# Embedding of the four prompt tiles: one pass by column quarters in place of two passes by tile pairs

## What is computed

```python
def finish_layer(x, mla_o, gla_o, p_i, w):
    mix = jnp.concatenate([rmsnorm(mla_o, w["norm_mla_out"]), gla_o], -1) @ w["w_out"]
    h = x + mix
    h = h + peer(rmsnorm(h, w["norm_ffn"]), w)
    gate = jax.nn.sigmoid((rmsnorm(h, w["norm_ple"]) @ w["w_ple_gate"]).astype(F32)).astype(h.dtype)
    return h + gate * (p_i @ w["w_ple_proj"])
```

## Time and profile before

| | |
|---|---|
| median of 3 runs | 4336.06 us |
| span of the profiled execution | 4331.6 us |
| VectorE busy | 3288.1 us, 76% |
| TensorE busy | 2254.9 us, 52% |
| DMA moved | 1599.51 MB, mean 369 GB/s |
| gathered rows taken up | 1152 |

### The profile page before, as it was taken

The page is one execution under the profiler, slowest core; times in us unless marked ns, Lnnn a source line. Parts: engine busy times, 40 slices in busy tenths (PEclk is TensorE's granted clock), DMA queues, the critical chain, the costliest instruction groups (busy, mean ns, idle before and its releaser), DMA issues.

```text
span 4331.6 us, 24058 instructions
## 1 busy us (share of the span) xinstructions
PE 2254.9 (52%) x8238; PEld 1342.1 (31%) x8238; DVE 3288.1 (76%) x3700; ACT 522.0 (12%) x1098; POOL 2201.2 (51%) x1216
## 2 busy tenths in 40 slices
PE   8999815425899492779942457710000920000755
PEld 4456403213475131367731222710000410000322
DVE  0130699997667998868889856699999699988673
ACT  2220112122002001212212010000001000001001
POOL 0000365744332556468775653345667368877441
PEclk9999956657999796767865678955555965555877
DMA  8658789988997999989999899988989999999996
GB/s 294 250 223 287 303 357 364 422 323 335 424 423 299 422 424 414 353 356 365 406 374 360 347 400 413 405 345 339 399 365 405 424 415 422 422 407 422 424 408 234
DMA packets 261153, 1599.51 MB, mean 369 GB/s; under 512 B 27763, under 2 KB 49459, under 8 KB 91750
## 3 DMA queue, kind: packets, MB, share of 16 engines
q0 software_dynamic: 176064, 1268.30, 72.0%
q1 hardware_dynamic: 83078, 320.64, 19.5%
q10 hardware_dynamic: 1888, 9.03, 0.5%
HBM read 1554.75 MB, written 42.56 MB: 369 GB/s over the span
## 4 chain that ended last, share of the span: by engine, by line
PE 31%; DVE 30%; POOL 16%; DMA 13%; issue 7%; ACT 2%; SPq 0%; DVEq 0%; ACTq 0%; POOLq 0%
POOL ring L2549 16%; PE bank L826 14%; DVE ring L1968 11%; DVE total L1993 9%; DMA ring<-in_peer_v,idx_all 5%; DMA ring<-in_peer_u,idx_all 5%; PE bank L1251 4%; PE bank L1288 3%; PE bank L929 1%; PE bank L891 1%; PE bank L800 1%; PE bank L1079 1%; DMA front<-in_cache_kv_latent,page_rows 1%; DVE front L1744 1%; PE bank L1093 1%
## 5 line engine op out<-in xcount | busy, mean ns | idle before, releaser
L1993 DVE SCALAR_TENSOR_TENSOR total<-ring,gate_all,total 128x2048 f32<-128x2048 f32 x571 | 1341.8, 2350 | 188.0 <-DMA ring<-in_peer_v,idx_all 164.5
L2549 POOL DMA_INDIRECT ring<-in_peer_u,idx_all x576 | 1062.2, 1844 | 795.7 <-DVE total L1993 359.1
L2549 POOL DMA_INDIRECT ring<-in_peer_v,idx_all x576 | 1072.2, 1861 | 711.9 <-DVE total L1993 376.3
L1968 DVE CUSTOM_DVE_ANT_0 ring<-ring,xrow 128x2048 f32<-128x2048 f32 x576 | 1297.5, 2287 | 169.4 <-DMA ring<-in_peer_u,idx_all 167.5
L826 PE MATMUL bank<-front 128*128 128x512 f32 (+3 forms) x1920 | 838.3, 594 | 68.9 <-ACT front L2115 64.6
L800 PE MATMUL bank<-inv_diag,front 128*128 128x128 f32 (+1 forms) x304 | 61.9, 391 | 1159.3 <-DVE inv_diag L1378 1102.2
L826 PEld LDWEIGHTS bank<-front 128*128 128x128 f32 (+1 forms) x1920 | 338.4, 181 | 558.5 <-issue 554.5
L800 PEld LDWEIGHTS bank<-inv_diag,front 128*128 128x128 f32 (+1 forms) x304 | 58.9, 299 | 1164.2 <-DVE inv_diag L1378 1098.2
L1251 PE MATMUL bank<-front 128*128 128x128 f32 (+2 forms) x1536 | 257.0, 329 | 20.5 <-DMA front<-in_peer_w_q 17.4
L1251 PEld LDWEIGHTS bank<-front 128*128 128x128 f32 x1536 | 239.8, 192 | 39.3 <-DMA front<-in_peer_w_q 20.3
L2574 POOL DMA_DIRECT2D ring<-in_w_in x12 | 10.7, 894 | 342.8 <-PE bank L1288 239.6
(11 more groups left out here) (323 smaller groups left out, 2894.0 us busy)
## 6 DMA issues: line engine op xcount, KB each, us to landing
front<-in_w_in SPq DMA_DIRECT2D x64, 980.0 KB, 8.4
front<-in_w_out SPq DMA_DIRECT2D x48, 1024.0 KB, 9.1
front<-in_peer_w_q SPq DMA_DIRECT2D x48, 1024.0 KB, 13.3
front<-in_w_ple_gate SPq DMA_DIRECT2D x48, 1024.0 KB, 9.1
ring<-in_w_in POOLq DMA_DIRECT2D x12, 1960.0 KB, 10.5
front<-in_w_uq SPq DMA_DIRECT2D x6, 1536.0 KB, 10.7
ring<-in_peer_u,idx_all POOLq DMA_INDIRECT x576, 14.3
ring<-in_peer_v,idx_all POOLq DMA_INDIRECT x576, 16.0
```

The costliest lines, as they stand in the source:

```text
L1968: e.tensor_tensor_reduce(out=ring[:, b, :], in0=ring[:, b, :], in1=xrow[:, t % 2, :], scale=1.0, scalar=0.0, op0=ALU.mult, op1=ALU.add, ac ...
L1993: e.scalar_tensor_tensor(out=total, in0=ring[:, b, :], scalar=c1, in1=total, op0=ALU.mult, op1=ALU.add).then_inc(s("summed"), 1)
L2549: e.indirect_dma_start(out=ring[:, k % RING, :], out_offset=None, in_=a[("peer_u", "peer_v")[side]][0], in_offset=bass.IndirectOffsetOnAxi ...
```

## The change

Tiles 0 to 3 are embedded together: `PLE_GROUPS = [[0, 1, 2, 3], [4]]`. Their turned rows fill `XTp` (16 x 512 wide, over `XT` and slabs 0 and 1 of `W`), their rows lie in `Hp` (over `H`, `Y` and `G`). The gate weights come in four quarters of 512 columns, each quarter in five chunks: four of 4 x 128 rows x 512 columns (1 MB), one of the projection weights (0.5 MB). Two chunk buffers `Wq` (slabs 2 and 3 of `W`) alternate: chunk i is issued when chunk i-2 has been used. A quarter takes 4 banks, the next one the other 4. The sum over 2048 and the number of matmuls are as before; the gate weights are read twice in all.

Rows that no longer go by way of DRAM are the normed rows of tiles 1 and 3, which VectorE writes straight into `xrow` slot 1 (`keeps_rows`; for tile 1 it waits for `z_ahead_stored`, for tile 3 until tile 1's rows are stored), and the finished rows of tile 3, which VectorE's last addition writes into `Hp[:, 3]`. Two `xn` stores and loads and one `h2` store and load, 1 MB each, drop out. Outputs of the prompt leave in two halves of 1024 columns. All tables are new. Each piece is run through by five engines' lists; the core of the diff, with the tables cut to a line or two:

```diff
@@ -59,7 +59,9 @@
-PLE_GROUPS = [[0, 1], [2, 3], [4]]
+PLE_GROUPS = [[0, 1, 2, 3], [4]]
+QUARTERS, KQ = 4, 4
+QUARTER_CHUNKS = 16 // KQ + 1
@@ -141,42 +143,46 @@
-PAGES_BEFORE = [395, 395, 395, 402, 404, 414, 414, 426, 428, 440, 440, 451, 452, 462, 467, 476]
+PAGES_BEFORE = [
+    372, 380, 380, 380, 389, 395, 406, 416, 416, 430, 434, 446, 449, 459, 472, 472]
 ROWS_BEFORE = [
...
-    830, 831, 831, 831, 831, 831, 837, 837, 840, 844, 844, 869, 878, 878, 879, 879, 879, 879, 879, 883, 883, 1073, 1073,
-    1083, 1083, 1123, 1123, 1123, 1123, 1123, 1124, 1124, 1124, 1124, 1124]
...
+    1019, 1026, 1033, 1041, 1047, 1054, 1079, 1079, 1079, 1081, 1098, 1104, 1104, 1112, 1120, 1128, 1135, 1138,
+    1138, 1138, 1138, 1138]
...
@@ -321,7 +327,17 @@
-    return 16 * (n // SLABS + 1 + (n >= PASSES[f"out{AHEAD}"]))
+    return 16 * (n // SLABS + 1 + (n >= PASSES[f"out{AHEAD}"]) - (n >= PASSES["gate1"]) * QUARTERS * QUARTER_CHUNKS // SLABS)
+CHUNKS_LANDED = ("half_w_loaded", "old_keys_loaded")
+CHUNKS_BEFORE = (16 * 3 * 2 * len(GROUPS), 16 * 3 * 2 * LAST)
+EMBEDDING_ROWS = [("rows_loaded", ROWS_IN["ffn", LAST] + 16), ("gain_loaded", 16 * len(GROUPS) + 16),
+                  ("ahead_rows_loaded", 16 * MT + 16)]
+def quarter_landed(i):
+    return s(CHUNKS_LANDED[i % 2]), CHUNKS_BEFORE[i % 2] + 16 * (i // 2 + 1)
@@ -347,6 +363,11 @@
+XTp = carve(KD, PT * P, at=0)
+Wq = [W[:, 2, :], W[:, 3, :]]
+Hp = carve(PT, D, at=h0)
+sigq, pTq, p_one = carve(PT, BANK, at=y0 + 2 * D), carve(PLE // P, PT * P), carve(PLE)
@@ -438,6 +459,14 @@
+def keeps_rows(t):
+    return t < PT and t % 2 == 1
+def normed_rows(t):
+    return xrow[:, t % 2, :] if keeps_rows(t) else Y
@@ -530,10 +559,10 @@
-                e.wait_ge(s("slabs_used"), n - SLABS + 1)
+                e.wait_ge(s("slabs_used"), max(n - SLABS + 1, PASSES["gate1"] if name == "gate1" else 0))
...
-            i = (k - PLE // P) % (KD + PLE // P) if name == "gate2" else k
+            i = (k - PLE // P) % (KD + PLE // P) if name == "gate1" else k
@@ -709,6 +738,8 @@
+                if keeps_rows(t):
+                    continue
@@ -745,22 +776,52 @@
+    def prompt_embedding_loads():
+        first = PASSES["gate0"]
+        def rows_of(t):
+            if t < PT - 1:
...
+                e.dma_start(Hp[:, t, :], h2_dram[rows(t), :]).then_inc(s(EMBEDDING_ROWS[t][0]), 16)
+            if t:
+                e.wait_ge(s("pT_ple_psum"), t)
+            e.dma_start(p_one, a["p_prompt"][0, 0][rows(t), :]).then_inc(s("p_loaded"), 16)
+        def chunk_of_gate(i):
+            q, c = i // QUARTER_CHUNKS, i % QUARTER_CHUNKS
+            e.wait_ge(s("slabs_used"), first + max(0, i - 1))
+            cols = slice(q * BANK, (q + 1) * BANK)
+            w, nk = (a["w_ple_gate"][0][c * KQ * P:(c + 1) * KQ * P, cols], KQ) if c < QUARTER_CHUNKS - 1 \
+                else (a["w_ple_proj"][0][:, cols], PLE // P)
+            e.dma_start(Wq[i % 2][:, 0:nk * BANK].rearrange("p (k n) -> p k n", k=nk), w.rearrange("(k p) n -> p k n", p=P))\
+                .then_inc(s(CHUNKS_LANDED[i % 2]), 16)
+        rows_of(0)
+        chunk_of_gate(0)
+        chunk_of_gate(1)
+        for t in range(1, PT):
+            rows_of(t)
+        for i in range(2, QUARTERS * QUARTER_CHUNKS):
+            if i == 3 * QUARTER_CHUNKS + 2:
+                prompt_embedding_stores(0)
+            chunk_of_gate(i)
+    def prompt_embedding_stores(half):
+        e.wait_ge(s("embedded"), PT * 2 * (half + 1))
+        cols = slice(half * D // 2, (half + 1) * D // 2)
+        for t in range(PT):
+            e.dma_start(o["y_p"][0][rows(t), cols], Hp[:, t, cols]).then_inc(s("y_out"), 16)
+    def sample_embedding_loads():
+        def between():
+            prompt_embedding_stores(1)
+            e.dma_start(p_row[:NS, 0, :], tile_of(a["p_prompt"][0, 0], a["p_sample"][0], PT)).then_inc(s("p_loaded"), 16)
+        slabs("gate1", a["w_ple_gate"][0], extra=a["w_ple_proj"][0], between=between)
+        e.wait_ge(s("embedded"), EMBEDDED[1] + 4)
+        e.dma_start(tile_of(o["y_p"][0], o["y_s"], PT), H[:NS, 0, :]).then_inc(s("y_out"), 16)
@@ -833,30 +894,44 @@
+    def prompt_embedding():
+        for t in range(PT):
+            now(norm_transposes("ple", [t]))
+            e.wait_ge(s("p_loaded"), 16 * (t + 1))
+            if t:
+                e.wait_ge(s("pT_ple_sb"), t)
+            for k in range(PLE // P):
+                mm = e.transpose(bank[5][:, k * P:(k + 1) * P], p_one[:, k * P:(k + 1) * P], ident[:, :])
+            mm.then_inc(s("pT_ple_psum"), 1)
+        e.wait_ge(s("nt_evacuated"), 4 * (NORMS["ple", PT - 1] + 1))
+        e.wait_ge(s("pT_ple_sb"), PT)
+        for q in range(QUARTERS):
+            banks = bank[PT * (q % 2):PT * (q % 2 + 1)]
+            for c in range(QUARTER_CHUNKS - 1):
+                i = q * QUARTER_CHUNKS + c
+                e.wait_ge(*quarter_landed(i))
+                for k in range(c * KQ, (c + 1) * KQ):
+                    for t in range(PT):
+                        if k == 0 and q >= 2:
+                            e.wait_ge(s("embedded"), PT * (q - 2) + t + 1)
+                        mm = e.matmul(banks[t][:, :], XTp[:, k, t * P:(t + 1) * P], Wq[i % 2][:, k % KQ * BANK:(k % KQ + 1) * BANK],
+                                      start=(k == 0), stop=(k == KD - 1))
+                mm.then_inc(s("slabs_used"), 1)
+            i = q * QUARTER_CHUNKS + QUARTER_CHUNKS - 1
+            e.wait_ge(*quarter_landed(i))
+            for t in range(PT):
+                e.wait_ge(s("sigmoid_ready"), PT * q + t + 1)
...
+                    mm = e.matmul(banks[t][:, :], pTq[:, k, t * P:(t + 1) * P], Wq[i % 2][:, k * BANK:(k + 1) * BANK],
+                                  start=(k == 0), stop=(k == PLE // P - 1))
+                mm.then_inc(s("embed_psum" if t < PT - 1 else "slabs_used"), 1)
...
+        R, n0, m0 = NS, PASSES["gate1"], 4 * NORMS["ple", PT]
...
+        e.wait_ge(s("embedded"), EMBEDDED[1])
@@ -1381,7 +1442,12 @@
-            e.scalar_tensor_tensor(out=Y[:R, 0:width], in0=H[:R, sl, 0:width], scalar=inv, in1=G[:R, 0:width],
+            if keeps_rows(t):
+                if t == GROUPS[AHEAD][0]:
+                    e.wait_ge(s("z_ahead_stored"), 16 * MT * AHEAD_RING // 2)
+                else:
+                    e.wait_ge(s("h2_stored"), 16 * (t - 1))
+            e.scalar_tensor_tensor(out=normed_rows(t)[:R, 0:width], in0=H[:R, sl, 0:width], scalar=inv, in1=G[:R, 0:width],
@@ -1880,27 +1946,28 @@
+    def prompt_embedding():
+        yield
+        yield from norm_rows("ple", PLE_GROUPS[0])
+        for q in range(QUARTERS):
+            cols = slice(q * BANK, (q + 1) * BANK)
+            for t in range(PT):
+                yield
+                if t < PT - 1:
+                    e.wait_ge(s("embed_psum"), (PT - 1) * q + t + 1)
...
+                    e.wait_ge(s("slabs_used"), PASSES["gate0"] + (q + 1) * QUARTER_CHUNKS)
+                link(e.tensor_tensor(sigq[:, t, :], sigq[:, t, :], bank[PT * (q % 2) + t][:, :], ALU.mult))
+                e.tensor_tensor(Hp[:, t, cols], Hp[:, t, cols], sigq[:, t, :], ALU.add).then_inc(s("embedded"), 1)
...
@@ -1997,14 +2063,17 @@
+            e.tensor_tensor(Hp[:, t, :] if t == PT - 1 else xr, xr, total, ALU.add).then_inc(s("peer_done"), 1)
...
+                if keeps_rows(t):
+                    e.wait_ge(s("normed"), NORMS["ffn", t] + 1)
+                else:
+                    e.wait_ge(s("xrow_loaded0"), 16 * (t // 2 + 1 if t < PT else T - 1))
@@ -2055,14 +2125,12 @@
-            ready(t)
...
-                e.wait_ge(s("xn_stored"), 16 * t)
+            ready(t)
@@ -2310,7 +2378,7 @@
-        e.wait_ge(s("xn_stored"), 16 * (tiles[-1] + 1))
+        e.wait_ge(s("xn_stored"), 16 * (tiles[-1] // 2 + 1))
@@ -2383,40 +2451,41 @@
+    def prompt_embedding():
+        for t in range(PT):
+            yield from norm_squares("ple", [t], lambda t: e.wait_ge(s("peer_done"), PT) if t == PT - 1
+                                    else e.wait_ge(s(EMBEDDING_ROWS[t][0]), EMBEDDING_ROWS[t][1]))
+            yield
+            e.wait_ge(s("pT_ple_psum"), t + 1)
+            e.copy(pTq[:, :, t * P:(t + 1) * P], four(bank[5])[:, 0:2]).then_inc(s("pT_ple_sb"), 1)
+        for q in range(QUARTERS):
+            yield
+            e.wait_ge(s("slabs_used"), PASSES["gate0"] + q * QUARTER_CHUNKS + QUARTER_CHUNKS - 1)
+            for t in range(PT):
+                if q:
+                    e.wait_ge(s("embedded"), PT * (q - 1) + t + 1)
+                e.activation(sigq[:, t, :], bank[PT * (q % 2) + t][:, :], ACT.Sigmoid).then_inc(s("sigmoid_ready"), 1)
+        yield
...
@@ -2493,7 +2561,9 @@
+        if keeps_rows(t):
+            return
+        e.wait_ge(s("xn_stored"), 16 * (t // 2 + 1))
```

164 lines of the change are left out of this document (44 added, 120 removed), and 69 rows, old and new, of tables (CHAIN_BEFORE_PIECE, ROWS_BEFORE).

## The result

The change makes the kernel slower: 4393.31 us, median of 4 runs (4390.77 to 4395.34), against 4338.45 (4333.66 to 4344.02); ratio 1.0125, 95% interval 1.0110 to 1.0139. The forecast was 4270, with a range of 4230 to 4328 and a chance of 0.12 for slower. The profiled execution has a span of 4389.0 us, 57.4 more than before.

The account below looks back on a forecast made before the run. Rows were taken as bound by DMA at 2.5 us each at best, slower where weights share DMA or VectorE has other steps. −8 −55 −11 +8 = −66 gave span 4265.6, plus 4.5 for the median 4270; range 4230 to 4328.

Parts of the forecast that it names:

- Up to row 671: Start to row 671: half the DMA time saved (4) and a removed wait (4), together −8 us.
- rival E: No net change: new tables misfit by 15 us and more, or freed DMA is spent elsewhere; near 4336, chance 0.08.
- the wait of 4 us that I priced: Group 1's chain: tile 2's squares waited 4.05 us for tile 1's store; that wait goes, 4 of the −8.
- Rows 672 to 1040: Middle stretch, 1049 us: the pass for tiles 0 and 1 leaves, VectorE's idle falls to 40; 993, entered as −55.
- the spread: Middle stretch: sample's routing spread up to row 999 so the ring never runs full; counted within the 40 us idle.
- Tile 3's end to the last sum: Last rows, 354 us: gate pass of 308 us, then 14 rows in 34; 342 to 343, so −11.
- The 15: Gate pass: a chunk in 2 KB pieces lands 15 us after issue, bounds 7.1 and 21.4.
- rival B: Last stretch: chunks land within 13.8 us and are no limit, DMA needs 325; −29 for −11, 4252, chance 0.20.
- rival D: Last stretch: chunks take 30 us to land and hold up VectorE; +93 for −11, 4374, chance 0.10.
- The rule of the Trainium skill on whole packets: Gate pass: DMA engines switch queues only after whole packets, so chunks wait behind gathered rows; would give 4374, not 4270.
- The tail: After the last summed row, 72.7 us: the sample tile's projection starts later; +8, bounds 0 and +25.

Follow-up runs that it names:

- third kernel: The change with both chain tables, and the row, step and page tables up to row 672, as before the change: 4278.9 us, ratio 0.9843 to 0.9878.
- tenth experiment: The third kernel with the change's row numbers from row 205 to 671 alone, and its PAGES_BEFORE: 4329.6 us, ratio 0.9969 to 0.9991.
- experiment 11: The third kernel with each gate chunk read as 128 whole rows in 8 KB pieces, so wrong weights: 4266.1 us, ratio 0.9820 to 0.9854.
- seventh kernel: The third kernel with the last eight ROWS_BEFORE numbers changed and the sample's p rows loaded ahead of the outputs' second half: 4278.4 us.

## Why the prediction was wrong, point by point

**Up to row 671 (−8, bounds +15 and −25): this step failed.** Measured +106 in the profile (row 672 at 2962 for 2856). The step that failed is the price of the new tables: I wrote that "a misfit of the tables could as well cost 15", left it out of the sum, and gave rival E, the same misfit, 0.08, with no row behind either number. The runs showed 14 to 23 us for the chain tables and 92 to 100 for the row tables. The part that had to do with what was built came out as I put it: with the old tables row 672 is 3 us early in the third kernel and 8 on average over five, and the wait of 4 us that I priced is gone, 8.12 us before tile 2's turning for 12.07.

The missing step could have been worked from the trace of before and the two lists. In the list of the change the steps of the mixer of tiles 1 and 2 stand 12 to 22 rows earlier than before: the one at L1420 (L1486 after) at row 27 for 41, the MEMSET at row 103 for 125. In the trace of before, ScalarE and VectorE at the first of these:

```profile
620.85 0.48 ACT L2084 ACTIVATE ms<-ms,eps 128x1 f32<-128x1 f32 x2
```

```profile
625.29 0.16 DVE L1420 RECIPROCAL ms<-ms 128x1 f32<-128x1 f32 x1
```

The input was ready at 621.3, the step began at 625.3: 4 us to spare. Fourteen rows earlier are at least 14 × 2.5 = 35 us. A step with 4 us to spare that is moved 35 us ahead must wait, unless its input comes sooner as well; it waited 15.6. I had looked at whether VectorE was idle before such steps and not at how narrowly it was not.

Such a charge finds the places better than the sizes. Taken as the time from the new place to the input's arrival, both in the trace of before, it is 7, 28, 14 and 45 us for the four steps, and the kernel after waited 14, 16, 15 and 15: in a run that is moved as a whole the inputs move too. For the two routing steps of the tenth experiment it is 33 and 28 us (231 and 655 rows are done by 1285.8 and 2798.1, the inputs came at 1318.5 and 2826.0), and that kernel waited 31.9 and 30.3.

**Rows 672 to 1040 (−55): right,** −57 after and −60 in the third kernel, and for the reason given: VectorE is idle for 37 us in it, where the sum left 40. The split was half right: I had given the spread no row of its own, and it is 13 to 17 of the 60.

**Tile 3's end to the last sum (−11): off by 12.** The start was right (27 us to the first gate matmul, measured 25.7), so was the landing of a chunk that goes alone (15, measured 15.8) and TensorE's wait for it. Too small were the quarters: 67.2, 76.4, 80.8 and 69.2 us for 64.2 and three times 71.4. A quarter's third chunk waited 2.2 to 4.5 us where I had 1.2, and within the rows of the timeline two chunks took 29.65 us where 27.7 are unhindered. The pass took 294 us for 278, and what follows it to the last sum 36 for 37. A chunk issued while another was on its way took longer than 15 us, up to 20.4 beside gathers in the third kernel. The 15 was partly luck. I had put it between 21.4 and 7.1, and the 7.1 is no landing time but the distance between slabs of which several were on their way; from issue to landing those slabs took 22.8 us in the kernel before:

```profile
front<-in_peer_w_q SPq DMA_DIRECT2D x12, 1024.0 KB, 22.8
```

So the row that I gave for rival B does not speak for it, and the size of the pieces alone does not set the landing. Neither rival B came (experiment 11 shows how much of it longer pieces bring) nor rival D: landing in the pass stayed below its 25 us.

**The rule of the Trainium skill on whole packets** ("DMA: Bandwidth & Descriptors", section "Queues, rings and completion order") would, as I applied it, have made a chunk land at about 30 us and given 4374. The measured landing, 15.8, is against that use of it, and the slow result near its number has another cause. Experiment 11 agrees with that use in its direction only: the first chunk of a quarter landed in 9 us with the longer pieces.

**The tail (+8): right,** 80.3 for 72.7, and for the reason given, the later projection. TensorE waits 31.8 us for the sample's `p` rows, until 4304.9. That is ahead of the last sum at 4308.7, but the projection and the turning of the rows stand behind it in TensorE's list, and so the sum's turning (last line) begins 10.4 us after the sum:

```profile
4304.88 0.45 PE L937 MATMUL bank<-ident,front 64*128 64x64 f32 x2 [31.80 <-DMA front<-in_p_sample]
4305.68 9.76 PE L944 MATMUL bank<-front 128*64 128x512 f32 x16 [0.35 <-ACT front L2473]
4315.37 3.78 PE L951 MATMUL bank<-ident,xrow 64*128 64x64 f32 x32
4319.08 3.79 PE L955 MATMUL bank<-fold,total 128*128 128x64 f32 x32
```

In the kernel before it began at once:

```profile
4258.89 7.09 PE L880 MATMUL bank<-fold,total 128*128 128x64 f32 x32 [45.14 <-DVE total L1993]
```

The seventh kernel loads the `p` rows first, but behind a pass that ends 16 us later than in the third, and its turning still begins 12.7 us after the sum. Loading them first without that delay was not tried.

**Rivals and chances.** The result, slower by 55, lies outside the range. I gave 0.80 to faster, from cases about the embedding alone. The third kernel, the change with the old tables up to row 672, takes 4278.9 us, 1.4% below before and 9 us from the forecast, which had in effect been made for it. Of the other kernels that use the right weights none is clearly faster; the seventh has 4278.4.

## What to carry to other kernels

Where an order is written out as numbers, the new numbers are a part of the change with a price of their own, and a large one: list the steps that come earlier among the rows, read in the old trace when their input was ready and how much earlier the new place is. The difference tells where a wait will arise; it is near the size of the wait only where the input stays where it was. Here nine rows cost up to 32 us and twenty-two cost 15. Judge the numbers by the end time and not by a stretch, since two misplacements can cover each other there. And when such a list must change only behind a point, leave the numbers ahead of that point as they are.

## What was not expected

A wait taken out of a relay of engines comes back at the next steps: four waits of 57 us together, with their steps moved by 3 to 7 rows, gave 2 us. A stall can also help: while VectorE did not take rows, no gathers ran, and a slab or chunk landed in 15 us for 28, or in less than 8 for 16. And a transfer of 1 MB in 2 KB pieces beside full gather traffic landed in 15.8 us; the same bytes in 8 KB pieces saved 12.9 us of the whole kernel, although the DMA engines were as good as full either way.
